# Second half of the first expert product as 512 moving columns, and attention values computed by token

## The chip, the cores and the metric

One NeuronCore of a Trainium2 chip runs the whole program in one launch. The metric is device time in microseconds, the median of several executions. The program is a chain of transformer layers on 256 tokens of width 1024.

## The reference, cut to what matters

Two blocks run one after the other. The first (two feed-forward parts and a token mixer) is not touched. The second has two layers, each with attention and then a product over experts ("peer"). All of it is in 32-bit floats.

```python
proj = h @ w_in[l]
q, k, v, b_gate, c_gate, hc, gate_a, gate_c = jnp.split(proj, SPLIT_POINTS, axis=-1)
...
# peer: 16384 experts, 128 x 128; each token has 8 heads x 16 chosen ones
u = jnp.take(expert_u, xc["idx"], axis=0)
vv = jnp.take(expert_v, xc["idx"], axis=0)
a = jax.nn.gelu(jnp.einsum("td,thkd->thk", xc["h"], u))
return jnp.einsum("thk,thkd->td", xc["g"] * a, vv)
```

## The kernel before, in words

**Units.** All weights come as units of 128 x 1024 floats (512 KB), in one order that is fixed when the program is written, through a ring of three buffers filled by SP's queue. To keep float precision on TensorE each unit is split into two parts: ScalarE writes the upper part `w_hi` (helper `hi`, L473, three buffers), VectorE the rest `w_lo` (helper `lo`, L904, two buffers). The activations are split in the same way into `h_hi` and `h_lo`. `step(u)` on ScalarE issues `hi(u + 2)` and then waits until TensorE has used unit u; `step(u)` on VectorE issues `lo(u + 2)`, which itself waits until unit u is used. A product with a unit is `w_hi*h_hi + w_hi*h_lo + w_lo*h_hi`. In `product`, which `tile` calls, these are three matmuls of 256 columns (the tokens) for each of the 8 slices of 128 of the unit: 24 in all, L1788 and L1789 in turn and then eight of L1792.

**The experts.** Each layer computes, instead of gathering, the dense product of all tokens with all experts: 128 units of `expert_u` (called u units here), `gelu`, a multiplication with a matrix of gates, and 128 units of `expert_v` (v units). The u units 0 to 63 run while VectorE chooses the top 16; the results go to the four banks of `st`. The u units 64 to 127 use only two banks of `st`, since the other two take the gates. In this half VectorE and TensorE go in "turns" of mostly two units each: VectorE makes one-hot matrices for 8 tokens (`right` L1531, `weigh` L1541 three times, `left` L1546), TensorE multiplies them in 24 small matmuls (`token_gates`, L2307), and VectorE multiplies the gates into the experts of the first half (`multiply`, L1555). There are 32 such turns, in four sections of eight; the last turn of a section has one unit alone. The same turns run once more beside the first 64 v units, there for the gates of the second half, and VectorE also makes `act_lo` once for each unit (`lower`, L1561) after ScalarE's `act_hi` (`upper`, L847). A v unit is 12 matmuls of 512 columns, in which the weights are the moving operand and 128 tokens are the stationary one (`v_unit`, L2340 and L2347), into the four banks of `acc`. The banks of `acc` are free during all u units. The last v unit is written out in another order (L2363). ScalarE applies gelu from the bank (`gelu_of`, L816). The turns of u units begin after the chosen keys have been transposed by TensorE and copied (L840, L841, L1605 to L1610).

**The values.** In the attention of each layer the columns of v are units 8 to 11 of the input projection (`pairs`, with `p` 4 and 5). They come out with channels on partitions (`vt`), and TensorE turns them by 8 transposes at `p` 10 (L2191); ScalarE copies the result (`v2`, L744). A semaphore `v2` is waited for before the first use.

In layer 0 the input projection runs while the GpSimd queue loads further weights for VectorE's dot products (L969).

## Time and profile before

| what | us |
|---|---|
| median of 3 runs | 2872.48 (2870.70 to 2873.51) |
| the profiled execution | 2876.32 |
| its span | 2874.7 |
| TensorE busy in the span | 2818.9 |

A row of groups gives line, engine, operation, tiles and shapes, count, then busy time in us and mean ns of one, then the idle time before and what ended it. A matmul's shown duration includes its passage through the array, so successive ones overlap: the cost of one in a stream is the distance between two starts. In a timeline the first column is the start, the second the duration, and a merged row with "x8" covers eight instructions.

### The profile page before, as it was taken

How to read it: one execution, taken by the hardware profiler on the slowest of the kernel's cores; microseconds unless marked ns; L12 is line 12 of the kernel's file. 1: busy time of each engine (PE TensorE's matmuls, PEld its weight loads, DVE VectorE, ACT ScalarE, POOL GpSimd, SP SyncE). 2: the span in 40 equal slices, each digit the busy share in tenths (PEclk: the TensorE clock that was granted, in tenths of full speed). 3: DMA queues.
4: the chain of work that ended last, by engine and by line, in shares of the span. 5: the costliest groups of instructions: out<-in, count | busy, mean ns of one | idle time of the engine just before them, and what ended most of it. 6: DMA issues, size and time to landing. Idle time of an engine off the chain costs nothing.

```text
span 2874.7 us, 58146 instructions
## 1 busy us (share of the span) xinstructions
PE 2818.9 (98%) x22454; PEld 2638.8 (92%) x22454; DVE 2129.6 (74%) x3811; ACT 1334.0 (46%) x1988; POOL 150.6 (5%) x199
## 2 busy tenths in 40 slices
PE   6999999999999999999999999999999999999999
PEld 6999989999999999999988888899999999988887
DVE  6778765577776668877789977756578877799765
ACT  3445543354445554443444444545454443444454
POOL 0112114001110000000000000000000000000000
PEclk9999999999999999999999999999999999999999
DMA  8885451278865455554445488654455544444554
GB/s 326 307 307 181 148 190 38 83 239 303 287 250 177 151 198 184 184 169 156 161 164 167 168 282 287 213 162 146 165 175 183 176 162 160 161 165 169 183 191 154
DMA packets 150722, 551.42 MB, mean 192 GB/s; under 512 B 16720, under 2 KB 16976, under 8 KB 150224
## 3 DMA queue, kind: packets, MB, share of 16 engines
q1 hardware_dynamic: 127584, 464.05, 47.7%
q0 software_dynamic: 22176, 80.75, 8.2%
q8 instruction: 179, 2.93, 0.4%
q10 hardware_dynamic: 720, 3.17, 0.3%
q14 instruction: 63, 0.52, 0.1%
HBM read 546.86 MB, written 1.05 MB: 191 GB/s over the span
## 4 chain that ended last, share of the span: by engine, by line
PE 75%; PEld 18%; DVE 2%; DMA 2%; issue 1%; ACT 1%; PEldq 0%; SPq 0%; POOLq 0%; POOL 0%; DVEq 0%; ACTq 0%
PE acc L2340 15%; PE st L1788 13%; PE st L1792 12%; PE st L1789 12%; PE acc L2347 7%; PEld st L1788 3%; PE st L2307 3%; PEld st L1792 3%; PEld st L1789 3%; PEld acc L1788 2%; PEld acc L1792 2%; PEld acc L1789 2%; DMA ring<-weights 2%; PE acc L1788 1%; PE acc L1789 1%; PE acc L1792 1%
## 5 line engine op out<-in xcount | busy, mean ns | idle before, releaser
L904 DVE TENSOR_TENSOR w_lo<-ring,w_hi 128x1024 fp32r<-128x1024 f32 x860 | 1057.2, 1231 | 500.5 <-PE st L1792 314.3
L473 ACT ACTIVATE w_hi<-ring 128x1024 fp32r<-128x1024 f32 x860 | 899.8, 1050 | 174.1 <-DMA ring<-weights 114.1
L1788 PE MATMUL st<-h_hi,w_hi 128*128 128x256 f32 x3888 | 964.8, 286 | 1.4 <-ACT w_hi L473 1.4
L1789 PE MATMUL st<-h_lo,w_hi 128*128 128x256 f32 x3888 | 954.9, 283 | 0.0
L1788 PEld LDWEIGHTS st<-h_hi,w_hi 128*128 128x128 f32 x3888 | 746.3, 192 | 11.0 <-issue 7.4
L1789 PEld LDWEIGHTS st<-h_lo,w_hi 128*128 128x128 f32 x3888 | 746.7, 192 | 0.0
L1792 PE MATMUL st<-h_hi,w_lo 128*128 128x256 f32 x3888 | 547.1, 283 | 3.3 <-DVE w_lo L904 3.3
L1792 PEld LDWEIGHTS st<-h_hi,w_lo 128*128 128x128 f32 x3888 | 502.2, 192 | 3.8 <-DVE w_lo L904 3.7
L2340 PE MATMUL acc<-w_hi,act_hi 128*128 128x512 f32 x1016 | 319.7, 396 | 2.0 <-ACT w_hi L473 2.0
L2340 PE MATMUL acc<-w_hi,act_lo 128*128 128x512 f32 x1016 | 313.4, 390 | 0.0
L816 ACT ACTIVATE arena<-st 128x256 f32<-128x256 f32 x256 | 98.5, 385 | 422.1 <-PE st L1792 421.8
L847 ACT ACTIVATE act_hi<-arena 128x256 fp32r<-128x256 f32 x256 | 106.8, 418 | 397.9 <-PE acc L2347 394.8
L2347 PE MATMUL acc<-w_lo,act_hi 128*128 128x512 f32 x1016 | 271.5, 389 | 0.0
L2340 PEld LDWEIGHTS acc<-w_hi,act_lo 128*128 128x128 f32 x1016 | 190.8, 188 | 41.0
L2347 PEld LDWEIGHTS acc<-w_lo,act_hi 128*128 128x128 f32 x1016 | 190.7, 188 | 39.6
L2340 PEld LDWEIGHTS acc<-w_hi,act_hi 128*128 128x128 f32 x1016 | 185.6, 188 | 37.8 <-issue 2.8
L1561 DVE TENSOR_TENSOR act_lo<-arena,act_hi 128x256 fp32r<-128x256 f32 x256 | 108.0, 423 | 79.9 <-ACT act_hi L847 79.8
L969 DVE SCALAR_TENSOR_TENSOR arena<-arena,extra 128x1024 f32<-128x1024 f32 x120 | 145.7, 1218 | 12.4 <-DMA arena<-ada_weights 12.1
L1541 DVE TENSOR_TENSOR extra<-extra 128x512 bf16<-128x512 bf16 x384 | 139.3, 418 | 0.0
L2307 PEld LDWEIGHTS st<-extra 128*128 128x128 bf16 x3072 | 99.8, 97 | 20.6 <-issue 16.7
L2307 PE MATMUL st<-extra 128*128 128x64 bf16 x3072 | 115.1, 193 | 0.8 <-DVE extra L1546 0.8
L1788 PE MATMUL acc<-act_hi,w_hi 128*128 128x256 f32 x424 | 104.1, 283 | 0.0
(334 smaller groups left out, 2874.2 us busy)
## 6 DMA issues: line engine op xcount, KB each, us to landing
ring<-weights SPq DMA_DIRECT2D x864, 512.0 KB, 3.4
arena<-ada_weights POOLq DMA_DIRECT2D x104, 512.0 KB, 5.7
extra<-ada_weights POOLq DMA_DIRECT2D x48, 512.0 KB, 4.5
arena<-ada_weights SPq DMA_DIRECT2D x16, 512.0 KB, 13.4
arena<-const ACTq DMA_DIRECT2D x1, 2112.0 KB, 12.0
x_t<-params SPq DMA_DIRECT2D x1, 1024.0 KB, 11.5
extra<-crows POOLq DMA_DIRECT2D x2, 512.0 KB, 5.4
out<-arena SPq DMA_DIRECT2D x4, 256.0 KB, 2.2
```

What stands on the lines that cost most here:

```text
L473: nc_a.activation(w_hi[:, u % 3, :], ring[:, u % RING, :], ACT.Copy).then_inc(hi_ready, 1)
L847: nc_a.activation(act_hi[:, n % 2, :], src, ACT.Copy).then_inc(sem("gated_hi"), 1)
L904: v.tensor_tensor(w_lo[:, u % 2, :], ring[:, u % RING, :], w_hi[:, u % 3, :], ALU.subtract)\
L969: v.scalar_tensor_tensor(out=w, in0=w, scalar=1.0, in1=c_row, op0=ALU.mult, op1=ALU.mult, accum_out=col).then_inc(ada_taken, 1)
L1541: ins = v.tensor_tensor(hot_r[b][k], hot_r[b][0], spread(gate_parts[:, k, :], g, i, HALF), ALU.mult)
L1561: v.tensor_tensor(act_lo[:, n % 2, :], src, act_hi[:, n % 2, :], ALU.subtract) .then_inc(sem("gated_lo"), 1)
L1788: mm(dst(t), w, hi_t(t), start=start, stop=False, skip_group_check=True)
L1789: mm(dst(t), w, lo_t(t), start=False, stop=False, skip_group_check=True)
L1792: ins = mm(dst(t), w_lo[:, u % 2, t * P:(t + 1) * P], hi_t(t), start=False, stop=last and (t == DT - 1 or not shared), skip_group_check=True)
L2307: ins = mm(st[:, 2 + g % 2, k * HALF:(k + 1) * HALF], hot_l[g % 2][:, k // 2, :, k % 2], hot_r[g % 2][part_][:, k // 2, :, k % 2], start=p ...
L2340: mm(acc[:, 2 * t + half, :], act_part[:, b, t * P:(t + 1) * P], w_hi[:, u % 3, 512 * half:512 * half + 512], start=n == 0 and i is None a ...
L2347: ins = mm(acc[:, 2 * t + half, :], act_hi[:, b, t * P:(t + 1) * P], w_lo[:, u % 2, 512 * half:512 * half + 512], start=False, stop=False, ...
```

## The change

`h_hi` and `h_lo` become the two halves of one buffer `h_both`, next to each other for each slice. For the u units 64 to 127 (`FOLDED`) of each layer, `wide` streams both halves as 512 columns against `w_hi` into a whole bank, in place of two matmuls of 256; `w_lo` still multiplies `h_hi` alone. The bank then holds two halves, which have to be added: ScalarE copies the second half to SBUF (`other_half`), VectorE adds the first half from the bank (`fold`), and ScalarE's gelu reads the sum from SBUF. The units 64 to 123 use the four banks of `acc`, the last four the banks 0 and 1 of `st`; a bank is free when its unit is folded. In the loop over most u units of both halves, ScalarE issues `hi(n + 3)` ahead of gelu n. TensorE waits for the fold of unit 123 before the first v unit.

The four value units are stored by rows of the weight and multiplied by `token_unit`, with the tokens stationary: 12 matmuls of 512 columns. The result has the layout of `v2` at once, in banks 0 and 1 of `acc`; ScalarE moves it out after `p` 5. The transposes, the buffer `vt`, the copy L744 and the waits on `v_tok` and `v2` go.

```diff
-        h_hi = sb("h_hi", [P, DT, T], F32R)
-        h_lo = sb("h_lo", [P, DT, T], F32R)
+        h_both = sb("h_both", [P, DT, 2, T], F32R)
+        h_hi, h_lo = h_both[:, :, 0, :], h_both[:, :, 1, :]
...
+        FOLDED = [n for n in range(NKEYS) if n >= HALF]
+        def u_place(n):
+            if n < HALF:
+                return st[:, u_bank(n), :]
+            return acc[:, n % 4, :] if n < NKEYS - 4 and n in FOLDED else st[:, n % 2, :]
...
-                        dst = vt[:, 2 * p - 8:2 * p - 6, :]
+                        dst, src = v2[:, p - 4, :], acc[:, p - 4, :]
...
-                    evict(p)
+                    if p == 5:
+                        evict(4)
+                    if p != 4:
+                        evict(p)
                     if p == N_EARLY // 2 - 2:
-                        eng.wait_ge(sem("v_tok"), l + 1)
-                        nc_a.activation(v2, acc[:, 0:2, :], ACT.Copy).then_inc(sem("v2"), 1)
                         exps(0)
...
-                    nc_a.activation(dst, st[:, u_bank(n), 0:T], ACT.Gelu_apprx_tanh).then_inc(sem("gelu"), 1)
+                    src = u_place(n)[:, 0:T]
+                    if n in FOLDED:
+                        src = dst
+                        eng.wait_ge(sem("folded"), fold_count(l, n) + 1)
+                    nc_a.activation(dst, src, ACT.Gelu_apprx_tanh).then_inc(sem("gelu"), 1)
+                def other_half(n):
+                    if n in FOLDED:
+                        nc_a.activation(experts[:, n, :], u_place(n)[:, T:2 * T], ACT.Copy).then_inc(sem("u_other"), 1)
                 def u_half(first, between=None, behind=None):
                     step(base + first)
+                    other_half(first)
                     for n in range(first, first + HALF - 4):
+                        hi(base + n + 3)
                         gelu_of(n)
                         step(base + n + 1)
+                        other_half(n + 1)
...
+                def fold(n):
+                    if n in FOLDED:
+                        eng.wait_ge(sem("u_other"), fold_count(l, n) + 1)
+                        v.tensor_tensor(experts[:, n, :], u_place(n)[:, 0:T], experts[:, n, :], ALU.add)\
+                            .then_inc(sem("folded"), 1)
...
                     right(half, g, i)
                     step(u, i, 4)
+                    fold(HALF + n)
                     weigh(half, g, i)
                     if g > 0:
                         multiply(half, g - 1, i)
                     left(half, g, i)
                     if not alone:
                         step(u + 1, i, 4)
+                        fold(HALF + n + 1)
...
+            def wide(bank, u):
+                eng.wait_ge(hi_ready, nth(u))
+                for t in range(DT):
+                    mm(bank, w_hi[:, u % 3, t * P:(t + 1) * P], h_both[:, t, :, :].rearrange("p a t -> p (a t)"),
+                       start=t == 0, stop=False, skip_group_check=True)
+                eng.wait_ge(taken, u + 1)
+                for t in range(DT):
+                    ins = mm(bank[:, 0:T], w_lo[:, u % 2, t * P:(t + 1) * P], h_hi[:, t, :], start=False,
+                             stop=t == DT - 1, skip_group_check=True)
+                ins.then_inc(used, 1)
...
+            def token_unit(u, n):
+                eng.wait_ge(hi_ready, nth(u))
+                for low in range(2):
+                    if low == 1:
+                        eng.wait_ge(taken, u + 1)
+                    for j in range(2):
+                        w = (w_lo[:, u % 2] if low else w_hi[:, u % 3])[:, 512 * j:512 * j + 512]
+                        for t in range(TT):
+                            for part_ in (h_hi,) if low else (h_hi, h_lo):
+                                ins = mm(acc[:, t, :], part_[:, 2 * n + j, t * P:(t + 1) * P], w,
+                                         start=not low and (n, j) == (0, 0) and part_ is h_hi,
+                                         stop=low == 1 and (n, j) == (3, 1), skip_group_check=True)
+                ins.then_inc(used, 1)
...
                 def u_tile(n, i=None):
-                    if n >= 4:
-                        eng.wait_ge(sem("gelu"), n_key + n - (3 if n < HALF - 2 else 1))
-                    tile(st[:, u_bank(n), 0:T], base + n)
+                    def freed(m):
+                        if m in FOLDED:
+                            eng.wait_ge(sem("folded"), fold_count(l, m) + 1)
+                        else:
+                            eng.wait_ge(sem("gelu"), n_key + m + 1)
...
+                    if n in FOLDED:
+                        wide(u_place(n), base + n)
+                    else:
+                        tile(u_place(n)[:, 0:T], base + n)
...
                 turns(0, lambda n, i=None: u_tile(HALF + n, i), selected)
+                eng.wait_ge(sem("folded"), fold_count(l, NKEYS - 4))
                 turns(1, v_unit)
```

## Rows read from the trace of the kernel before

**Rows 1.** The page's first part: busy time by engine.

```profile
PE 2818.9 (98%) x22454; PEld 2638.8 (92%) x22454; DVE 2129.6 (74%) x3811; ACT 1334.0 (46%) x1988; POOL 150.6 (5%) x199
```

**Rows 2.** Waits of TensorE over the whole span, longest first.

```profile
PE st L1846 <- ACT arena L503: 17.3, 3, 16.8
```

**Rows 3.** Stretches: us, then busy us (instructions) of PE, PEld, DVE, ACT, POOL; clock; DMA.

```profile
1254.00:1454.00 200.00, 200.00 (x2203) 198.67 (x2202) 154.27 (x250) 81.81 (x123) 0.00 (x0) 1.00 0.48 162
1454.00:1650.00 196.00, 196.00 (x1508) 160.13 (x1508) 176.86 (x314) 84.16 (x124) 0.00 (x0) 1.00 0.50 167
```

**Rows 4.** Timeline of TensorE in the second half of the first product, one turn.

```profile
1262.98 0.28 PE L1788 MATMUL st<-h_hi,w_hi 128*128 128x256 f32 x1
...
1264.90 1.12 PE L1792 MATMUL st<-h_hi,w_lo 128*128 128x256 f32 x8
1265.86 0.90 PE L2307 MATMUL st<-extra 128*128 128x64 bf16 x24
...
1272.43 0.90 PE L2307 MATMUL st<-extra 128*128 128x64 bf16 x24
```

**Rows 5.** Chain of waits, two v units without gates: start, us, what.

```profile
1668.56 1.81 PE acc L2340 x8
1671.28 1.81 PE acc L2340 x8
```

**Rows 6.** Timeline of TensorE, last unit of the second product.

```profile
1830.36 0.39 PE L2363 MATMUL acc<-w_hi,act_lo 128*128 128x512 f32 x1
1830.58 0.39 PE L2363 MATMUL acc<-w_lo,act_hi 128*128 128x512 f32 x1
```

**Rows 7.** Timeline of all engines, one turn of the second product.

```profile
1492.18 0.42 DVE L1561 TENSOR_TENSOR act_lo<-arena,act_hi 128x256 fp32r<-128x256 f32 x1
...
1492.52 0.68 DVE L1546 TENSOR_TENSOR extra<-extra 128x1024 bf16<-128x1024 bf16 x1
...
1494.07 0.90 PE L2307 MATMUL st<-extra 128*128 128x64 bf16 x24
...
1500.37 0.90 PE L2307 MATMUL st<-extra 128*128 128x64 bf16 x24
```

**Rows 8.** Groups by line, 1254 to 1450 us.

```profile
L473 ACT ACTIVATE w_hi<-ring 128x1024 fp32r<-128x1024 f32 x59 | 62.0, 1051 | 2.2 <-DMA ring<-weights 2.2
...
L816 ACT ACTIVATE arena<-st 128x256 f32<-128x256 f32 x59 | 22.8, 386 | 114.6 <-PE st L1792 114.6
L1555 DVE TENSOR_TENSOR arena<-arena,st 128x512 f32<-128x512 f32 x32 | 21.7, 679 | 3.9 <-PE st L2307 3.9
```

**Rows 9.** Groups by line, whole span.

```profile
L1561 DVE TENSOR_TENSOR act_lo<-arena,act_hi 128x256 fp32r<-128x256 f32 x256 | 108.0, 423 | 79.9 <-ACT act_hi L847 79.8
L847 ACT ACTIVATE act_hi<-arena 128x256 fp32r<-128x256 f32 x256 | 106.8, 418 | 397.9 <-PE acc L2347 394.8 <-DVE arena L1555 3.1
...
L1028 DVE TENSOR_TENSOR arena<-arena,st 128x256 f32<-128x256 f32 x44 | 18.2, 414 | 2.6 <-PE st L1792 2.6
```

**Rows 10.** Timeline at the start of the folded half, VectorE and then TensorE.

```profile
1249.83 1.22 DVE L904 TENSOR_TENSOR w_lo<-ring,w_hi 128x1024 fp32r<-128x1024 f32 x1
1250.96 1.09 DVE L1541 TENSOR_TENSOR extra<-extra 128x512 bf16<-128x512 bf16 x3
1251.97 0.68 DVE L1546 TENSOR_TENSOR extra<-extra 128x1024 bf16<-128x1024 bf16 x1
...
1252.71 0.90 PE L2307 MATMUL st<-extra 128*128 128x64 bf16 x24 [0.40 <-DVE extra L1546]
```

**Rows 11.** Timeline of TensorE around the values' transposes, layer 0.

```profile
868.27 1.13 PE L1792 MATMUL st<-h_hi,w_lo 128*128 128x256 f32 x8
...
872.02 1.12 PE L1792 MATMUL st<-h_hi,w_lo 128*128 128x256 f32 x8
```

**Rows 12.** Timeline of ScalarE and TensorE, the input projection of layer 0.

```profile
849.67 1.06 ACT L473 ACTIVATE w_hi<-ring 128x1024 fp32r<-128x1024 f32 x1 [1.87 <-DMA ring<-weights]
...
850.99 1.12 PE L1792 MATMUL st<-h_hi,w_lo 128*128 128x256 f32 x8
```

More of the change, by code:

```diff
@@ L286, in build @@
         pt_b = [ar(14344, 384), ar(14728, 384)]
-        vt = ar(15112, 4, T)
         stat = ar(16136, 8, 8)
@@ L396, in u_bank, with fold_count @@
             return n % 4 if n < HALF - 4 else n % 2
+        FOLDED = [n for n in range(NKEYS) if n >= HALF]
+        def fold_count(l, n):
+            return len(FOLDED) * l + sum(f < n for f in FOLDED)
+        def u_place(n):
+            if n < HALF:
+                return st[:, u_bank(n), :]
+            return acc[:, n % 4, :] if n < NKEYS - 4 and n in FOLDED else st[:, n % 2, :]
         def quarter(banks, r):
@@ L830, in u_half @@
                             step(base + n + 1)
+                            other_half(n + 1)
                 def gates_exp():
@@ L1416, in pace @@
                         step(base + paced["units"])
+                        fold(paced["units"])
                         paced["units"] += 1
@@ L1611, in _ @@
                 turns(0, u_turn)
-                step(base + NKEYS - 4)
-                step(base + NKEYS - 3)
+                for n in (NKEYS - 4, NKEYS - 3):
+                    step(base + n)
+                    fold(n)
                 multiply(0, TURNS - 1)
@@ L1616, in _ @@
                 lower(1)
-                step(base + NKEYS - 2)
-                step(base + NKEYS - 1)
+                for n in (NKEYS - 2, NKEYS - 1):
+                    step(base + n)
+                    fold(n)
                 turns(1, v_turn)
@@ L1918, in _, with pairs @@
             stage(eng, ST["ffn0"])
-            def pairs(base, n, sem_name, before, fresh, ahead=None):
+            def token_unit(u, n):
[11 more added lines that the diff above has]
+                ins.then_inc(used, 1)
+            def pairs(base, n, sem_name, before, fresh, ahead=None, by_token=()):
                 for p in range(n):
@@ L1924, in pairs @@
                         ahead(p)
+                    if p in by_token:
+                        for k in range(2):
+                            token_unit(base + 2 * p + k, 2 * (p - by_token[0]) + k)
+                        continue
                     if p >= 4:
@@ L2185, in ahead @@
                 def ahead(p):
-                    if p == N_EARLY // 2 - 2:
-                        eng.wait_ge(sem("proj2"), 20 * l + 6)
-                        for t in range(TT):
-                            for n in range(4):
-                                ins = nc.tensor.transpose(acc[:, t, n * P:(n + 1) * P], vt[:, n, t * P:(t + 1) * P], ident)
-                        ins.then_inc(sem("v_tok"), 1)
                     if p == N_EARLY // 2 - 1:
@@ L2195, in ahead @@
                         scores_of(0)
-                pairs(U + O_QK, N_EARLY // 2, "proj2", 20 * l, 3 + 2 * l, ahead)
+                pairs(U + O_QK, N_EARLY // 2, "proj2", 20 * l, 3 + 2 * l, ahead, by_token=(4, 5))
                 eng.wait_ge(sem("proj2"), 20 * l + N_EARLY // 2 - 2)
@@ L2202, in _ @@
                     gate_unit(2 * h)
-                    if h == 0:
-                        eng.wait_ge(sem("v2"), l + 1)
                     turned(h)
@@ L2276, in u_tile @@
                 def u_tile(n, i=None):
-                    if n >= 4:
-                        eng.wait_ge(sem("gelu"), n_key + n - (3 if n < HALF - 2 else 1))
-                    tile(st[:, u_bank(n), 0:T], base + n)
+                    def freed(m):
[3 more added lines that the diff above has]
+                            eng.wait_ge(sem("gelu"), n_key + m + 1)
+                    if n < HALF:
+                        if n >= 4:
+                            freed(n - (4 if n < HALF - 2 else 2))
+                    elif n not in FOLDED:
+                        freed(n - 2)
+                    elif n < NKEYS - 4:
+                        if n >= HALF + 4:
+                            freed(n - 4)
+                    else:
+                        freed(n - 2 if n >= NKEYS - 2 else n - HALF - 2)
+                    if n in FOLDED:
+                        wide(u_place(n), base + n)
+                    else:
+                        tile(u_place(n)[:, 0:T], base + n)
                 for n in range(HALF):
@@ L2400, in _two_tiles, with _token_tiles @@
     return w.reshape(4, P, 4, 2, P).transpose(2, 1, 3, 0, 4).reshape(-1, P, UNIT)
+def _token_tiles(w):
+    return w.reshape(4, 2, P, 512).transpose(0, 2, 1, 3).reshape(-1, P, UNIT)
 def _row_tiles(w):
@@ L2467, in _weights @@
         put(U + O_QK, tiles[0:8])
-        put(U + O_V, tiles[8:12])
+        put(U + O_V, _token_tiles(a["w_in_2"][l][:, 1024:1536]))
         put(U + O_REST, np.concatenate([tiles[12:24], tiles[32:40], tiles[24:32]]))
```

## The prediction

> **What bounds the kernel now.** I read the page's first part, then the waits of TensorE, then the busy times of single stretches, and then timelines. TensorE is busy for 2818.9 of 2874.7 us [rows 1], and its longest waits lie at the norms between the stages, 17.3 us in three waits under the first heading [rows 2]: nothing of the change is there. In the u units 64 to 127 of layer 0, TensorE is busy through the whole stretch, 200.00 of 200 us, and in the gated half of the v units for 196.00 of 196, at a granted clock of 1.00, which is the 2.4 GHz level [rows 3]. VectorE is busy for 154.27 of those 200 us and ScalarE for 81.81. So here each ns off the matmul stream shortens the end, as long as VectorE keeps up. What is to be seen in the timeline is the distance of starts. Sixteen matmuls of 256 columns take from 1262.98 to 1264.90, 0.120 us each [rows 4]. A v unit of twelve matmuls of 512 columns takes 1671.28 - 1668.56 = 2.72 us, 0.227 us each [rows 5]. 256 columns more therefore cost 0.107 us, and each matmul carries a fixed part of 0.120 - 0.107 = 0.013 us. The v unit alternates between banks; the last one sends three in a row to the same bank, and there the distance is 0.22 to 0.23 us too [rows 6], so a stream of 512 columns into one bank as in `wide` should have this pace.
>
> **The wide units.** A u unit now has 24 x 0.120 = 2.88 us. Afterwards it has eight of 512 and eight of 256: 8 x 0.2267 + 8 x 0.120 = 2.77 us. The number of columns is the same (6144); eight fixed parts go, 0.107 us a unit. For 128 units (64 in each of two layers): 13.7 us off TensorE. Bounds: nothing, if a wide matmul costs two narrow ones (0.240 us); and 13.7 us, since the columns remain.
>
> The page "TensorE: Matmul & The Clock Gate" of the Trainium skill, in its section "Back-to-back issue gap", gives an isolated gap of N/2.4 + 2.5 ns, so 109.2 ns for 256 columns and 215.8 for 512. By that rule a pair would lose 2.5 ns, not 13, the 128 units 2.6 us, and the whole sum below would be 4.6 us; the rows above, 120 and 227 ns, disagree with it for this kernel's operands, and I go by them.
>
> **What VectorE and ScalarE get.** Per folded unit ScalarE gets one copy of 128x256 out of a bank, near the gelu's 386 ns [rows 8], and its gelu now reads SBUF, near the 418 of L847 [rows 9]. A turn of two units then gives it 2 x (1.05 + 0.39 + 0.42) = 3.7 us. VectorE gets one addition of 128x256 with one operand in a bank: L1028 has this form at 414 ns [rows 9]. A turn before lasts 1272.43 - 1265.86 = 6.57 us [rows 4]; afterwards 6.57 - 0.21 = 6.36. VectorE is busy for 154.27 / 200 x 6.57 = 5.07 us in a turn; with two additions at most 5.07 + 0.83 = 5.90, and 5.75 when they overlap their neighbours as L1561 does: its next instruction starts 0.34 us behind its own start [rows 7]. Both are below 6.36. The better evidence is the turn of v units. There VectorE does the same turn with two `lower` of 423 ns in place of the two additions, each waiting for a ScalarE result too, and the turn lasts only 1500.37 - 1494.07 = 6.30 us [rows 7], with TensorE busy for 196.00 of 196 us [rows 3]. So the additions are covered by VectorE's idle time of 1.5 us a turn. If that cover is gone, each 0.1 us over 6.36 in a turn costs 6.2 us (62 turns in the two layers, the first of each apart).
>
> The order inside a turn holds as well. In VectorE's stream the next start lies some 0.08 us before the shown end: 1.13 us behind `lo`, 1.01 behind the three of `weigh` [rows 10]; so I take 0.60 for `left` and `multiply`, shown at 0.68 and 0.679 [rows 8, 10], and 0.34 for `right` and the additions. `fold(n)` waits for the copy of unit n, but stands behind `lo(n + 2)`, which starts when unit n is used and takes 1.13 us, longer than the copy. Behind it wait `weigh`, `multiply` and `left`. `left` ends 1.13 + 0.34 + 1.01 + 0.60 + 0.60 = 3.7 us after the first unit of the turn is used; TensorE wants it one group of gates and two units later. The gates take 6.57 - 2 x 2.88 = 0.81 us, so that is at 0.81 + 5.55 = 6.36 us. ScalarE's gelu(n) waits for `folded`, and behind it the copy of n + 1, which is why it matters that `hi(n + 3)` stands ahead: the split of the next weights doesn't hang on VectorE. The second addition of a turn ends near 5.2 us, its gelu near 5.6, and the next copy can't begin before its unit is done at 6.4. TensorE reuses a bank of `acc` four units later, far behind. In the first half of the u units, which isn't folded, gelu(n) comes later by one `hi` of 1.05 us, or by a late transfer; but unit n + 3 needs that `hi` anyway, and the bank is wanted only for unit n + 4: nothing. No transfer is added; SP's queue sees the same 512 KB a unit, at 162 GB/s in this stretch [rows 3].
>
> **Where the gain is not whole: the entry.** The first gates of the folded half wait 0.40 us for `left` at 1252.71 [rows 10]. Before that lie `lo` at 1249.83, `weigh` and `left`, all on VectorE and without a gap. The copy of unit 64 is done by then. `fold(64)` comes between `lo` and `weigh`: 0.34 us later (0.41 at most). The three units ahead of the gates are shorter by 0.32 us; of this the chain of VectorE gains only the 0.11 of unit 64. So the first gates start 0.23 us later instead of 0.32 earlier, a loss of 0.55 us a layer, 1.1 us in both. At the other end TensorE waits for fold 123 with four units in between, and the units 126 and 127 for the folds two units back: nothing. The first v unit starts 4 x 2.77 + 2 x 0.81 = 12.7 us after unit 123, and its `act_hi` and `act_lo` follow the last `multiply`, which can start at 2 x 2.77 + 2 x 0.81 = 7.2 us and is followed by 0.60, 0.42 and 0.34 us on the two engines, with `lo` units at most 2.3 more.
>
> **The values.** Four units a layer go from 2.88 to twelve matmuls of 512, 2.72 us: 8 x 0.16 = 1.3 us. The eight transposes go: between the two rows of `w_lo` around them lie 872.02 - 868.27 = 3.75 us instead of 2.88, so 0.87 us a layer, 1.7 in both [rows 11]. The copy L744 and the wait for it go from ScalarE, off the path. The two evictions move behind `p` 5, ScalarE has one eviction more there at once; the split of the next weights then waits for its transfer anyway. In layer 0 this stretch is short of transfers: at 849.67 ScalarE had waited 1.87 us for the ring, ended at 850.73, and TensorE wants that split when it has done the eight of 850.99, at 851.95 [rows 12]. That lead of 1.2 us is more than the 0.64 us which four shorter units take from it. If it weren't, 0.6 us of the 1.3 would be lost.
>
> **The sum.** 13.7 - 1.1 + 1.3 + 1.7 = 15.6 us. The profiled execution took 2876.32 us, afterwards 2860.7; against the median of the three runs, 2872.48, that is **2856.9 us** (0.54% less). No change that can be measured is one within 0.2%, 5.7 us.
>
> **The rivals.**
>
> A. *VectorE becomes the bound (slower).* Place: the turns of the folded half. If the copies of ScalarE are not hidden behind `lo`, each unit costs VectorE the copy and a handover too: 5.07 + 2 x (0.41 + 0.39 + 0.10) = 6.87 us a turn. It decides from 6.36 us a turn on, and makes the kernel slower from 6.62 on (6.57 and the 3.0 us of the values over 62 turns). At 6.87: 62 x 0.30 - 3.0 = 15.6 us slower, 2888 us. For it: VectorE is near 90% busy in the v turns, 176.86 of 196 us. Against it: those very turns, which carry the same load at 6.30 us without a wait of TensorE. Chance 0.05.
>
> B. *The fixed part is not saved, or only a little of it.* If the 13 ns hang on something that a wide stream of `h_both` has twice, or are mostly saved already, the wide units bring 0 to 2.6 us and the values 3.0 less the entry 1.1: 1.9 to 4.5 us, 2868 to 2871 us, not to be told from before. For it: the only streams of 512 columns in the trace have weights as the moving operand. Against it: the pace is 0.227 in all of them. Chance 0.08; the page's rule above belongs here.
>
> C. *Part is given back inside the sections.* A turn with one unit takes TensorE 2.77 + 0.81 = 3.6 us but VectorE 1.13 + 0.34 x 2 + 1.01 + 0.60 x 2 = 4.0. The deficit of about 0.45 us is caught up in the next turns, which leave at least 6.36 - 5.90 = 0.46 us each. If it isn't, TensorE loses it eight times: 3.6 us, 2860.5 us. For it: VectorE has to wait for used units as well. Against it: the v turns show no such wait. Chance 0.09.
>
> The forecast itself has the remaining 0.78.
>
> **How the numbers follow.** The forecast's own bounds: an addition of 0.41 rather than 0.34 in the entries, 0.1 us; 0.6 us in layer 0; some 2 us either way for transfers that fall otherwise in the stage where both queues load; 2 to 3 us between medians, since the three runs shown spread over 2.8 us. That gives 2853.5 to 2861. C lies inside it. Up to 2865 takes in the half of C with a larger loss; A and B, 0.13 together, and a little from the edges stay out. Faster by over 0.2%: forecast and C, 0.87. Within 0.2%: B, 0.08. Slower: A, 0.05.
>
> **What the changed profile would show.** The rows of `wide` with starts 0.227 us apart, and 2.77 us a unit; a turn of 6.36 us between two groups of gates; TensorE busy through the folded half, with no wait for VectorE in it except one of about 0.95 us before the first gates in each layer; `fold` at about 414 ns x128, the copy at about 386 x128; L744 and L2191 gone; TensorE with 22454 - 1024 - 112 = 21318 matmuls. What would make it wrong: a start distance of 0.24 us in `wide`; TensorE waiting for `left` or for `w_lo` in each turn; a VectorE that sits idle before `fold` for ScalarE's copy.

## The result, and the profile after

The changed kernel takes 2857.59 us (median of 5 runs, 2856.63 to 2858.12); the kernel before, on the same chip, 2871.55 (2870.68 to 2873.51). The ratio is 0.995, with a 95% interval of 0.9939 to 0.9961: 14.0 us or 0.49% less. The forecast was 2856.9, or 15.6 us less.

The page's first part for the changed kernel, beside [rows 1]:

```profile
PE 2802.8 (98%) x21318; PEld 2576.2 (90%) x21318; DVE 2166.8 (76%) x3939; ACT 1385.7 (49%) x2114; POOL 150.6 (5%) x199
```

TensorE has the 21318 matmuls that the forecast counted. Its profiled execution took 2857.49 us, 18.8 less than that of before. Some 5 of the 18.8 lie outside both parts of the change: the short stretches at the lower granted clock fell otherwise (about 3 us; in 500 to 560 us the granted clock is 0.97 instead of 0.94, in 920 to 970 us 1.00 instead of 0.97), the first stages of the program are 0.5 us earlier, the wait ahead of layer 0's attention is 0.7 us shorter, and in the v units of layer 0 TensorE waited 2.0 us for `w_hi` before and 0.6 now. So I read differences between marks of the same stage, not positions.

**The folded half.** The groups of the new code, whole span (for a group: busy us, mean ns of one, then the idle time before and what ended it):

```profile
L1841 PE MATMUL acc<-h_both,w_hi 128*128 128x512 f32 x960 | 244.8, 397 | 0.0
L1845 PE MATMUL acc<-h_both,w_lo 128*128 128x256 f32 x960 | 133.8, 282 | 0.0
L833 ACT ACTIVATE arena<-arena 128x256 f32<-128x256 f32 x128 | 53.5, 418 | 74.6 <-DVE arena L1445 74.6
L1445 DVE TENSOR_TENSOR arena<-acc,arena 128x256 f32<-128x256 f32 x120 | 50.3, 419 | 0.0
L839 ACT ACTIVATE arena<-acc 128x256 f32<-128x256 f32 x120 | 45.8, 382 | 107.7 <-PE acc L1845 107.4
```

The addition takes 419 ns and the copy 382 (forecast 414 and 386; the other eight of each are the units in `st`). ScalarE idles 74.6 us before its gelus, waiting for additions. The addition itself has no idle time ahead of it: VectorE never sits before `fold` for ScalarE's copy. The same stretch as in [rows 3], shifted to the changed kernel:

```profile
core 0: us, PE busy (x) PEld busy (x) DVE busy (x) ACT busy (x) POOL busy (x), PEclk, DMA share, GB/s
1252.00:1446.00 194.00, 194.00 (x1712) 172.62 (x1711) 170.42 (x307) 105.21 (x182) 0.00 (x0) 1.00 0.50 166
```

TensorE is busy for 194.00 of 194 us, at a granted clock of 1.00, with VectorE up to 170.42: the load of VectorE grew and TensorE has no visible wait. A matmul's shown duration can hide a short wait, but the starts show none: the gates start 121 or 122 ns after the narrow matmul ahead of them, in both kernels and in every group but the first of each layer. From the first gates to the first v unit the stage took 1454.42 - 1252.71 = 201.71 us before (the first gates of [rows 10] and TensorE's first start on `act_hi`) and takes 1443.69 - 1247.47 = 196.22 now; in layer 1 it is 196.21 instead of 201.70. That is 5.49 us a layer, where 61 units with 0.107 us each would be 6.5. The chain of waits shows why it is less (start, us, engine, tile, line, count; a stretch counts up to the next one's start):

```profile
1251.25 1.84 PE acc L1841 x8
1253.09 0.95 PE acc L1845 x8
1254.04 0.73 PE st L2390 x24
1254.78 1.91 PE acc L1841 x8
1256.68 0.95 PE acc L1845 x8
1257.64 1.84 PE acc L1841 x8
```

A unit is 1.84 + 0.95 = 2.79 us, and 1.91 + 0.95 = 2.86 behind the gates, where the forecast has 2.77. The starts one by one, worked out from the trace, in ns from each start to the next (wide is a matmul of 512 columns, narrow one of 256):

```
wide, behind eight narrow:  233 236 228 233 231 227 227 227
narrow, behind eight wide:  113 119 120 120 120 120 120 120
wide, behind the gates:     314 232 231 227 227 227 227 227
all narrow (before):        120 120 120 120 120 120 120 120
narrow behind gates (before): 201 118 118 120 120 120 120 120
```

The pace is 227 and 120, as forecast, but every change from narrow to wide costs 6 + 9 + 1 + 6 + 4 = 26 ns more, of which the change back returns 7 + 1. By the sums of these starts a unit saves 2.880 - 2.794 = 0.086 us, and behind gates 2.957 - 2.864 = 0.093, instead of 0.107.

**The turn.** TensorE's timeline at two groups of gates that bound a turn in the middle of the folded half:

```profile
1308.62 0.90 PE L2390 MATMUL st<-extra 128*128 128x64 bf16 x24
1309.36 2.07 PE L1841 MATMUL acc<-h_both,w_hi 128*128 128x512 f32 x8
1311.27 1.11 PE L1845 MATMUL acc<-h_both,w_lo 128*128 128x256 f32 x8
1312.22 2.00 PE L1841 MATMUL acc<-h_both,w_hi 128*128 128x512 f32 x8
1314.06 1.11 PE L1845 MATMUL acc<-h_both,w_lo 128*128 128x256 f32 x8
1315.02 0.90 PE L2390 MATMUL st<-extra 128*128 128x64 bf16 x24
```

6.40 us from gates to gates (forecast 6.36, before 6.57 by [rows 4]). Between the first and the last gates of a layer lie 28 such turns and three of one unit. By the starts of all gates of layer 0 the 28 take 6.39 us each and the three 3.60 (before 6.57 and 3.69): no turn stands out.

**The entry.** VectorE's timeline ahead of the first gates of layer 0, then TensorE's row, as in [rows 10]:

```profile
1244.26 1.22 DVE L931 TENSOR_TENSOR w_lo<-ring,w_hi 128x1024 fp32r<-128x1024 f32 x1
1245.39 0.42 DVE L1445 TENSOR_TENSOR arena<-acc,arena 128x256 f32<-128x256 f32 x1
1245.73 1.09 DVE L1577 TENSOR_TENSOR extra<-extra 128x512 bf16<-128x512 bf16 x3
1246.73 0.69 DVE L1582 TENSOR_TENSOR extra<-extra 128x1024 bf16<-128x1024 bf16 x1
1247.47 0.91 PE L2390 MATMUL st<-extra 128*128 128x64 bf16 x24 [0.73 <-DVE extra L1582]
```

The addition stands between `lo` and `weigh` and moves `left` by 0.34 us. The shown wait is 0.73 us instead of 0.40. A second, shorter one doesn't show in the rows, since the matmul before it covers it: around the first `w_lo` matmul of unit 66 the starts are 408 and 223 ns apart, against 227 and 113 in a unit that doesn't wait (before 159 and 223, against 120 and 120), 0.15 us more than before. The two together make 0.48 us a layer. From the first matmul of unit 64 to the first gates it is 10.22 us now and was 9.97 before, in both layers: the gates come 0.25 us later, where the forecast has 0.23.

**The values.** TensorE's timeline of token units:

```profile
831.91 2.00 PE L1984 MATMUL acc<-w_hi,h_both 128*128 128x512 f32 x8
833.76 1.07 PE L1984 MATMUL acc<-w_lo,h_both 128*128 128x512 f32 x4
834.66 1.98 PE L1984 MATMUL acc<-w_hi,h_both 128*128 128x512 f32 x8
```

A unit takes 834.66 - 831.91 = 2.75 us (forecast 2.72); the transposes of [rows 11] and their copy are gone.

### The profile page after: what moved, and what is told of

It reads as the page before. It is cut to its first block, busy times and chain, and to the rows that moved or that the text cites. A ratio compares the mean times of both kernels' runs of the same rounds, so it can differ in the third digit from the quotient of the medians.

```text
span 2855.8 us, 56114 instructions
## 1 busy us (share of the span) xinstructions
PE 2802.8 (98%) x21318; PEld 2576.2 (90%) x21318; DVE 2166.8 (76%) x3939; ACT 1385.7 (49%) x2114; POOL 150.6 (5%) x199
## 3 DMA queue, kind: packets, MB, share of 16 engines
q8 instruction: 170, 2.79, 0.4%
## 4 chain that ended last, share of the span: by engine, by line
PE 75%; PEld 18%; DVE 2%; DMA 2%; issue 1%; ACT 1%; PEldq 0%; SPq 0%; POOLq 0%; ACTq 0%; POOL 0%; DVEq 0%
PE acc L2423 16%; PE st L1828 8%; PE st L1832 8%; PE st L1829 8%; PE acc L2430 8%; PE acc L1841 8%; PE acc L1845 4%; PEld st L1828 3%; PE st L2390 3%; PEld st L1832 3%; PEld st L1829 3%; PEld acc L1828 2%; PEld acc L1832 2%; PEld acc L1829 2%; DMA ring<-weights 1%; PE acc L1828 1%
## 5 line engine op out<-in xcount | busy, mean ns | idle before, releaser
L1828 PE MATMUL st<-h_both,w_hi 128*128 128x256 f32 x2800 | 691.5, 285 | 0.7 <-ACT w_hi L485 0.7
L1829 PE MATMUL st<-h_both,w_hi 128*128 128x256 f32 x2800 | 686.9, 283 | 0.0
L1828 PEld LDWEIGHTS st<-h_both,w_hi 128*128 128x128 f32 x2800 | 536.9, 192 | 10.6 <-issue 7.4
L1829 PEld LDWEIGHTS st<-h_both,w_hi 128*128 128x128 f32 x2800 | 537.2, 192 | 0.1
L1832 PE MATMUL st<-h_both,w_lo 128*128 128x256 f32 x2800 | 394.1, 283 | 3.2 <-DVE w_lo L931 3.2
L1832 PEld LDWEIGHTS st<-h_both,w_lo 128*128 128x128 f32 x2800 | 361.6, 192 | 3.6 <-DVE w_lo L931 3.6
L1841 PE MATMUL acc<-h_both,w_hi 128*128 128x512 f32 x960 | 244.8, 397 | 0.0
L1841 PEld LDWEIGHTS acc<-h_both,w_hi 128*128 128x128 f32 x960 | 172.0, 189 | 30.3
L1845 PEld LDWEIGHTS acc<-h_both,w_lo 128*128 128x128 f32 x960 | 130.8, 190 | 10.1 <-DVE w_lo L931 0.9
L1845 PE MATMUL acc<-h_both,w_lo 128*128 128x256 f32 x960 | 133.8, 282 | 0.0
## 6 DMA issues: line engine op xcount, KB each, us to landing
x_t<-params SPq DMA_DIRECT2D x1, 1024.0 KB, 11.5
```

Source lines behind the costliest of these rows:

```text
L1828: mm(dst(t), w, hi_t(t), start=start, stop=False, skip_group_check=True)
L1829: mm(dst(t), w, lo_t(t), start=False, stop=False, skip_group_check=True)
L1832: ins = mm(dst(t), w_lo[:, u % 2, t * P:(t + 1) * P], hi_t(t), start=False, stop=last and (t == DT - 1 or not shared), skip_group_check=True)
L1841: mm(bank, w_hi[:, u % 3, t * P:(t + 1) * P], h_both[:, t, :, :].rearrange("p a t -> p (a t)"), start=t == 0, stop=False, skip_group_check ...
L1845: ins = mm(bank[:, 0:T], w_lo[:, u % 2, t * P:(t + 1) * P], h_hi[:, t, :], start=False, stop=t == DT - 1, skip_group_check=True)
```

## The experiments

Each time is the median of that kernel's runs, and each ratio is to the kernel before on the same chip. "After" is the changed kernel with 14.0 us less than before.

**1. The values alone.** No unit is folded; values by token stay, and so does `hi(n + 3)` ahead of the gelu.

```diff
-        FOLDED = [n for n in range(NKEYS) if n >= HALF]
+        FOLDED = []
...
-                eng.wait_ge(sem("folded"), fold_count(l, NKEYS - 4))
```

> The changed kernel with no u unit folded: only the value units by token remain, with the transposes gone. My account gives 3.0 us less than the kernel before (8 x 0.16 us for the units, 2 x 0.87 us for the transposes), about 2868.5 us where before takes 2871.5. If the transposes and the value units lay beside other work, the time would be that of before (2871.5), and the wide units would have brought all 14 us.

2868.12 us (2864.93 to 2871.88), ratio 0.9988 (0.9979 to 0.9997): 3.5 us less than before. The forecast's two terms for the values make 3.0. That leaves 10.5 us for the folded units, where the sum has 13.7 - 1.1 = 12.6. The turns of this run last 6.57 and 3.69 us, as in the kernel before, so the new place of `hi(n + 3)` alone brings nothing there.

**2. The gelu ahead of the next split.** In `u_half` the line `hi(base + n + 3)` ahead of `gelu_of(n)` goes; the split is then made in `step`, behind the gelu, as before.

```diff
                     for n in range(first, first + HALF - 4):
-                        hi(base + n + 3)
                         gelu_of(n)
```

> The changed kernel without the line that issues hi(n + 3) ahead of gelu n, so that the split of the next weights stands behind the gelu, which waits for the fold. Theory one (the prediction said the place of this line matters): ScalarE hangs on VectorE, the split of unit n + 3 comes up to 3.7 us later, w_lo behind it is late and TensorE waits in the turns: 0.2 us or more a turn, 12 us slower than the changed kernel. Theory two: by my own times of a turn the second gelu ends near 5.6 us and the split behind it near 6.65, while VectorE asks for it at 6.4 and has 0.8 us to spare: within 1 us of the changed kernel (2857.6).

2881.33 us, ratio 1.0033 (1.0021 to 1.0046): 23.7 us slower than after, and slower than before. The timelines of ScalarE and VectorE in one turn, and TensorE's two rows of gates:

```profile
1306.90 0.42 ACT L833 ACTIVATE arena<-arena 128x256 f32<-128x256 f32 x1 [2.04 <-DVE arena L1444]
1307.22 1.04 ACT L485 ACTIVATE w_hi<-ring 128x1024 fp32r<-128x1024 f32 x1
...
1306.45 0.42 DVE L1444 TENSOR_TENSOR arena<-acc,arena 128x256 f32<-128x256 f32 x1
1306.78 0.42 DVE L1566 TENSOR_TENSOR extra<-extra 128x512 bf16<-128x512 bf16 x1
1308.30 1.23 DVE L930 TENSOR_TENSOR w_lo<-ring,w_hi 128x1024 fp32r<-128x1024 f32 x1 [1.10 <-ACT w_hi L485]
...
1305.45 0.90 PE L2389 MATMUL st<-extra 128*128 128x64 bf16 x24
1312.12 0.90 PE L2389 MATMUL st<-extra 128*128 128x64 bf16 x24
```

There is a closed loop: addition (1306.45), gelu (1306.90), split on ScalarE (1307.22 to 1308.26), split on VectorE (1308.30), the next addition behind it. VectorE idles 1.10 us in it, more than the 0.78 us that it has to spare in a turn of the changed kernel (experiment 6), so `left` is late: the gates of both rows start 380 ns after the narrow matmul ahead of them instead of 122. The turn lasts 6.67 us instead of 6.39, those of one unit 4.01 instead of 3.60: 2 x (28 x 0.28 + 3 x 0.41) = 18 us of the 23.7, the rest before and behind these turns. The loop decides, and my estimate that the split would catch up within 1 us was wrong.

**3. Wide and narrow in pairs.** In `wide` the narrow matmul of part t stands right behind the wide one, but for units 65 to 67, whose `w_lo` comes late.

```diff
                 for t in range(DT):
-                    mm(bank, w_hi[:, u % 3, t * P:(t + 1) * P], h_both[:, t, :, :].rearrange("p a t -> p (a t)"),
-                       start=t == 0, stop=False, skip_group_check=True)
-                eng.wait_ge(taken, u + 1)
-                for t in range(DT):
-                    ins = mm(bank[:, 0:T], w_lo[:, u % 2, t * P:(t + 1) * P], h_hi[:, t, :], start=False,
-                             stop=t == DT - 1, skip_group_check=True)
+                    if paired:
+                        high(t)
+                    ins = low(t)
```

> In each folded unit but the second to fourth of a layer the eight wide matmuls and the eight narrow ones go in turn (wide 0, narrow 0, wide 1, ...) instead of first all wide, then all narrow; TensorE therefore waits for w_lo at the start of the unit. In the profile of the changed kernel a wide unit takes 2.795 us instead of 2.77: five starts after the narrow ones are 228 to 236 ns apart, and the first narrow one after the wide ones follows after 113 ns, the others after 120. Theory F (every matmul costs its columns and a fixed 13 ns): a pair costs 347 ns in any order, 2.77 us a unit, at most 0.02 us less than now: 0 to 3 us faster than the changed kernel. Theory W (the narrow stream is held at 120 ns by the loading of weights; a matmul alone needs 113 ns for 256 columns and 227 for 512): a pair costs 340 ns, a unit 2.72 us, about 0.075 us less than now in 122 units: 9 us faster, near 2848.5. Theory S (each change of width costs time): seven more changes a unit, each some 6 ns or more: 5 us slower or worse.

2859.94 us (2858.32 to 2862.93), ratio 0.996: 2.3 us slower than after. TensorE's timeline:

```profile
1300.60 0.40 PE L1841 MATMUL acc<-h_both,w_hi 128*128 128x512 f32 x1
1300.84 0.28 PE L1844 MATMUL acc<-h_both,w_lo 128*128 128x256 f32 x1
1300.96 0.40 PE L1841 MATMUL acc<-h_both,w_hi 128*128 128x512 f32 x1
```

From one wide start to the next a pair takes 361, 349 and 350 ns in turn in the unit behind the gates and mostly 347 in the other one (narrow starts of 113 to 120 ns, wide ones of 230 to 241), against 227 + 120 = 347. A full turn lasts 6.43 us instead of 6.39, 1.8 us in both layers. The narrow one is short behind a wide one and the wide one long behind a narrow one. Nothing can be gained by spreading the changes, and the guess that a pair would come down to 340 ns, with the load of a narrow one's weights hidden behind a wide stream, is refuted.

**4. The low part wide too.** The `w_lo` matmuls stream `h_both` as well (the product `w_lo` x `h_lo` is added, which the kernel leaves out), so no width changes inside a unit.

```diff
-                    ins = mm(bank[:, 0:T], w_lo[:, u % 2, t * P:(t + 1) * P], h_hi[:, t, :], start=False,
+                    ins = mm(bank, w_lo[:, u % 2, t * P:(t + 1) * P], h_both[:, t, :, :].rearrange("p a t -> p (a t)"),
+                             start=False, stop=t == DT - 1, skip_group_check=True)
```

> In the folded units w_lo is multiplied with both halves too, as 512 columns, so that a unit is sixteen wide matmuls and no narrow one (it computes one product more, w_lo x h_lo; the additions and copies stay). This is for the distances of starts. Theory N (the five long starts, 228 to 236 ns, follow from the narrow stream before): they vanish between units, all are 226 to 227, and remain only behind the gates. Theory C (the copy of ScalarE and the addition of VectorE, which work in the same first microsecond of a unit on banks of acc, slow TensorE's stream): they remain at the start of each unit. The time rises by 128 x 8 x 0.107 = 109 us over the changed kernel, near 2967, under N about 2 us less.

2966.7 us (one run; before beside it 2871.34). TensorE's timeline:

```profile
1303.71 1.98 PE L1845 MATMUL acc<-h_both,w_lo 128*128 128x512 f32 x8
1305.52 1.98 PE L1841 MATMUL acc<-h_both,w_hi 128*128 128x512 f32 x8
1307.34 1.98 PE L1845 MATMUL acc<-h_both,w_lo 128*128 128x512 f32 x8
```

Sixteen take 1307.34 - 1303.71 = 3.63 us, 0.227 each, and single starts are 226 to 227 apart also where `w_hi` gives way to `w_lo` or the bank changes. The long starts (318, 231, 236, 228, 233, 230) stand only behind the gates. So neither the bank, nor the source of the weights, nor a new unit, nor the copy and the addition that work on the banks at a unit's start makes them; what comes before them is always a run of narrower matmuls.

**5. Half the weight columns in the low part.** The `w_lo` matmuls load 64 of their 128 columns (the correction by `w_lo` is left out for the other half of each unit's rows).

```diff
-                    ins = mm(bank[:, 0:T], w_lo[:, u % 2, t * P:(t + 1) * P], h_hi[:, t, :], start=False,
+                    ins = mm(bank[0:64, 0:T], w_lo[:, u % 2, t * P:t * P + 64], h_hi[:, t, :], start=False,
```

> In the folded units each narrow matmul with w_lo takes only 64 of its 128 weight columns and writes 64 partitions (half of the w_lo correction of these units is left out). For the distances of starts again. Theory W (the narrow stream is held at 120 ns by the loading of 128 columns of weights; 256 moving columns alone need 113): the eight narrow starts come down to 113 ns and the first wide ones behind them are 227; 128 x (8 x 7 + 20) ns = 10 us faster than the changed kernel, near 2848. Theory F (a fixed part on each matmul): they stay at 120; the time stays at 2857.6. The run with pairs of wide and narrow ones spoke against W in its simple form, since a pair took 346 to 358 ns there.

2853.93 us (one run; before beside it 2871.34), where theory W had 2848. Narrow starts are now 113 to 118 ns apart, not 120: 113 is half of 227. So 120 is not 107 for the columns and a fixed 13 for each matmul: 7 of the 13 ns depend on the 128 columns of weights, or on the 128 partitions that are written, which the edit halves too. The first narrow matmul behind wide ones, with all 128 of both, has 113 as well, and that speaks for the loading, which can run ahead there. But the load alone isn't 120 either. In the changed kernel, at a granted clock of 1.00:

```profile
1045.69 4.51 PE L2335 MATMUL acc<-arena 128*128 128x128 f32 x38 [0.69 <-ACT arena L807]
```

These matmuls load 128 columns of weights each and stream only 128, and their starts are 111 to 112 ns apart (their operands are float32, those of the units float32r). The load by itself stays at 112, the stream of 256 by itself at 113, and the two together come to 120; no run shows why. The wide ones behind the narrow ones keep their transient, 232, 236, 228, 233, 231, against theory W, which had 227 for them.

**6. One and two more additions for each unit.** Idle additions of the same form, into a buffer that nobody reads then, are put ahead of the real one, for n below 126.

```diff
+                        for _ in range(1 if n < NKEYS - 2 else 0):
+                            v.tensor_tensor(act_lo[:, _, :], u_place(n)[:, 0:T], experts[:, n, :], ALU.add)
                         v.tensor_tensor(experts[:, n, :], u_place(n)[:, 0:T], experts[:, n, :], ALU.add)\
```

> A second, idle addition of the same form (its result is thrown away) ahead of each fold but the last two of a layer. VectorE gets 0.34 us more a unit. By the sum of a turn VectorE then has 5.49 + 0.68 = 6.17 us of work in a turn of 6.4: its cover holds, and only the entry costs 0.34 us more a layer, under 1 us (2858.5). Rival (VectorE has no idle time left, since it waits for the copy and for used units): 0.4 us or more a turn, 25 us slower.

> Two further idle additions ahead of each fold. VectorE then has 5.49 + 1.36 = 6.85 us in a turn, more than TensorE's 6.4: VectorE is the bound. 62 x 0.44 = 27 us slower than the changed kernel and 1 us more at the entries, near 2886. If the time stays within 10 us of the changed kernel, my sum of VectorE's turn is too high.

With one more: 2860.22 us (2859.26 to 2861.52), ratio 0.996, 2.8 us over after. With two more: 2894.26 (2892.67 to 2895.45), ratio 1.008, 36.9 us over after. The busy times of the stretch for the first, and then for the second with TensorE's wait (us, times, longest):

```profile
1254.00:1440.00 186.00, 186.00 (x1649) 165.63 (x1648) 184.19 (x360) 98.92 (x174) 0.00 (x0) 1.00 0.50 167
```

```profile
1254.00:1440.00 186.00, 177.03 (x1551) 153.34 (x1550) 186.00 (x384) 87.99 (x160) 0.00 (x0) 1.00 0.46 151
...
PE st L2393 <- DVE extra L1585: 21.7, 64, 1.4
```

With 184.19 of 186 us busy, VectorE still holds up nobody but the first gates (their wait grows to 1.1 us). With 186.00 of 186 it is the bound, TensorE waits at every group of gates, and the full turn lasts 6.80 us. The bound lies between one and two more. In the stretch of after VectorE has (194.00 - 170.42) / 194.00 x 6.39 = 0.78 us to spare in a turn; the starts of the idle additions and the real one lie 0.33 us apart, so one more in both units takes 0.66 and two take 1.3. For one more I expected 1 us; 0.6 are in the waits at the first gates (2.1 us in both layers instead of 1.5), the rest is within the spread. With two more a full turn is longer by 0.41 us and one of one unit lasts 4.67 instead of 3.60: 2 x (28 x 0.41 + 3 x 1.07) = 29 us of the 36.9, and 3.6 more are waits for the addition at the units in `st`. The expectation was too low since the turns of one unit, whose deficit full turns catch up while they have time to spare, then pay for themselves.

**7. All units folded.**

```diff
-        FOLDED = [n for n in range(NKEYS) if n >= HALF]
+        FOLDED = [n for n in range(NKEYS)]
```

> All 128 u units of a layer are folded, also those beside the choice of the top 16. Each of the 128 further units should save TensorE 0.087 us as in the turns: 11 us faster than the changed kernel, near 2846.5. Rival: VectorE gets 64 x 0.34 = 22 us more a layer in a stretch of which it was busy for 155.6 of 191 us, while the stretch gets 5.6 us shorter; it has then some 8 us left, and if the additions come at bad places (they follow the pacing of the other work, with ScalarE's copy to wait for) the choice is late and TensorE waits for it: no gain or some us slower.

2853.82 us, ratio 0.9938 (0.9924 to 0.9951): 3.8 us under after, of 11 expected. By TensorE's starts the units gain 0.087 us each, 5.1 us up to unit 60 of a layer; the next three give 3.4 us back. At units 62 and 63, where two banks are left for four, TensorE waits for the addition, 5.5 us in both layers:

```profile
1229.00 2.11 PE L1841 MATMUL st<-h_both,w_hi 128*128 128x512 f32 x8 [1.57 <-DVE arena L1445]
1230.95 1.11 PE L1845 MATMUL st<-h_both,w_lo 128*128 128x256 f32 x8
1233.26 2.11 PE L1841 MATMUL st<-h_both,w_hi 128*128 128x512 f32 x8 [1.21 <-DVE arena L1445]
```

A bank of a folded unit comes free a split, a copy and an addition after its use, not a gelu after. Here, in the last four units of a half, split, gelu and addition also follow each other as in experiment 2. With two banks that is too late in this place. It isn't in every one: the last four folded units of the changed kernel have two banks and the same order, and TensorE doesn't wait there. Which of the two decides was not tried.

**8. All but units 56 to 63, and without unit 64.** The second form also leaves 64, whose addition stands ahead of the first gates, narrow.

```diff
+        FOLDED = [n for n in range(NKEYS) if n < HALF - 8 or n >= HALF]
...
+        FOLDED = [n for n in range(NKEYS) if n < HALF - 8 or n > HALF]
```

> The folded units are 0 to 55 and 64 to 127. With all 128 folded, the trace shows the first 56 units gaining some 4 to 5 us a layer, and TensorE then waiting 1.57 and 1.21 us for folds in the units 62 and 63, which have two banks only, because the fold, the gelu and the split of the next weights follow each other there. Left narrow, these eight units should cost no wait: 56 x 0.087 = 4.9 us a layer, 9.7 us faster than the changed kernel, near 2848. If the gain of the first units is given back in another place (the choice of the top 16 late on VectorE), it ends near the 2853.8 of the kernel with all folded.

> As before it, and unit 64, the first of the turns, is not folded either, so that no addition lies between w_lo and the one-hot matrices of the first turn. The first gates should wait about 0.4 us instead of 0.73 and come 0.3 us earlier, against 0.09 us for the narrow unit: 0.5 us faster over both layers than the kernel with 0 to 55 and 64 to 127 folded, near 2847.5, which the times alone will hardly show; the wait before the first gates will.

2850.48 us (2847.34 to 2850.62), ratio 0.9919 (0.9906 to 0.9933), and 2849.69 (2846.1 to 2853.54), ratio 0.9922 (0.9908 to 0.9935). Both beat the changed kernel, by about 8 us where 9.7 was expected; they can't be told from each other by the time. Most of what is missing lies in layer 1: the units 0 to 55 gain 4.7 us in either layer by TensorE's starts, but at unit 62 of layer 1 TensorE loses 2.0 of them again, in both forms. It waits for a gelu that frees its bank, and ScalarE is late with that gelu: it has waited 2.64 us for a transfer and then makes the exponential of the gates (L862) between two table loads of 1.28 us. The changed kernel has the same two loads, but its split had no transfer to wait for there, and TensorE doesn't wait. The rows are those of the first form:

```profile
2242.83 1.06 ACT L485 ACTIVATE w_hi<-ring 128x1024 fp32r<-128x1024 f32 x1 [2.64 <-DMA ring<-weights]
2244.18 1.28 ACT L862 ACT_TABLE_LOAD   x1
2245.91 1.28 ACT L833 ACT_TABLE_LOAD   x1
2247.64 0.38 PE L1828 MATMUL st<-h_both,w_hi 128*128 128x256 f32 x1 [1.73 <-ACT arena L833]
```

By the trace the form without unit 64 removes the longer wait of the entry:

```profile
1242.18 0.90 PE L2390 MATMUL st<-extra 128*128 128x64 bf16 x24 [0.39 <-DVE extra L1582]
```

0.39 us, as in the kernel before; with unit 64 folded it is 0.7.

## Why the prediction was right

**The bound.** That TensorE's stream sets the end, and each ns off it shortens the end, held: TensorE busy for 194.00 of 194 us after.

**The wide unit: right mechanism, too large a size.** The term of 13.7 us was the step that was mis-sized. The paces were right, the change between them was left out: 5.49 us over 61 units is 0.090 a unit, 11.5 us over 128 units. Also wrong was the reading of 120 ns as 107 for the columns and 13 fixed. Experiment 5 shows 113 for 256 columns when half the weight columns are loaded, so a pair gains twice the 7 ns that a narrow matmul with 128 weight columns takes above this, less the transient. That reading didn't hurt the sum, since 227 and 120 came from rows.

**The page's gap.** The rule of the Trainium skill ("TensorE: Matmul & The Clock Gate", section "Back-to-back issue gap") is stated for an isolated matmul and would give 109.2 and 215.8 ns. The prediction's sum by it, 2.6 - 1.1 + 1.3 + 1.7, is 4.5 us, not the 4.6 written there, and near 3.4 when the value units too are priced by it (24 x 109.2 against 12 x 215.8 ns). The traces show 120 and 227, in both kernels, and 14.0 us; with 64 weight columns 113. The measurement decides against it for these operands.

**The entry.** This step held. From the start of `lo` to the gates it is 1247.47 - 1244.26 = 3.21 us, before 1252.71 - 1249.83 = 2.88 [rows 10]: the addition's 0.33. VectorE's chain gained only the 0.08 us of unit 64, so the gates come 0.25 us later (forecast 0.23), and the saving of the three units ahead of them, 3 x 0.09 us, is lost with it. That is 0.52 us a layer, where 0.55 was forecast.

**The values.** 3.0 us forecast, 3.5 measured by experiment 1 (its interval is 0.9 to 6.0); layer 1's attention shortened by 1.54 us in the trace, 1.5 forecast. The loss of 0.6 us for layer 0's transfers did not appear.

**The sum with the measured sizes.** 11.5 - 1.0 + 1.3 + 1.7 = 13.5 us, against 14.0 measured; the five runs of either kernel spread over 1.5 and 2.8 us. From unit 64 to the first v unit a layer takes 5.24 us less in the traces, 10.5 us in both, as experiment 1 leaves for the folded units. That the time itself, 2857.59, came within 0.7 us of the forecast 2856.9 is in part luck: the gain was 1.6 us smaller than forecast, and the kernel before has a median 0.9 us lower over five runs than over the three that the forecast started from.

**Rival A**, VectorE as the bound, is what experiment 6 produces with two additions more, and what experiment 2 produces by an order; the change stays 0.78 us a turn away from it. The step on the order inside a turn was right that `hi(n + 3)` ahead of the gelu matters. **Rival B** falls by the starts and by experiment 1: the folded units bring 10.5 us. **Rival C** did not happen: the turn behind each one-unit turn lasts 6.39 us like the others, and the gates never start late between the first ones and the v units.

**What stays open.** Why a stream of 512 columns takes five starts to reach its pace behind narrower ones. Experiments 3 to 5 exclude the bank, the source of the weights, the unit's border, the copy and the addition, and the width of the narrow ones' weights; what is left, the change of the streamed width itself, wasn't tried with other widths. It is open too why behind the gates two starts are long in the changed kernel (232, 231) after the first, and five in experiment 4. Nor is it known why 128 weight columns and 256 streamed ones take 120 ns together when neither takes more than 113 alone.

## What to carry to other kernels

Read the price of a matmul as the distance of starts at its own width and weight load, and look at the first starts behind a change of width too: here 18 of 107 ns a unit went there, in an otherwise right sum. Merging two streams with the same weights paid here because two short ones take 240 ns and the merged one 227; the merged halves must be joined, and that is free only while the joining engine has slack in each turn and its result is not awaited by a split that the same engine waits for. An addition that frees a bank makes the bank free later; where only two banks rotate, look at what else must happen before the next use. And look for waits in the starts too: a wait shorter than a matmul's shown duration is in no row of idle time.

## What the runs showed of the hardware

- A float32r matmul of 512 streamed columns follows the last after 227 ns. One of 256 follows after 120 ns with 128 weight columns and after 113 to 118 with 64 (and half the written partitions, experiment 5). Matmuls of 128 streamed and 128 weight columns (float32, L2335) follow after 111 to 112. A load's shown duration (189 and 190 ns in the groups of L1841 and L1845) is longer than these distances, so loads overlap each other and the streams.
- The first five wide starts behind narrow ones are 233, 236, 228, 233 and 231 ns; the first narrow one behind wide ones is 113.
- The first start behind the gates (64 columns, bf16) is 314 to 318 ns instead of 227 for a wide one, and 201 instead of 120 for a narrow one: some 80 to 90 ns more behind the gates, for the wide ones in the changed kernel and for the narrow ones in the kernel before.
- A wait of TensorE can be invisible in idle time: in experiment 2 the gates mostly start 377 to 399 ns after the matmul ahead of them instead of 122, and TensorE is shown idle before them for 8 groups only, 2.9 us in all.
